# A ring of raw weights with five places in place of six, and a ring of high parts with five in place of four

## The reference

```python
for l in range(2):                                   # first block
    h = rmsnorm(x, norm_g[l])
    (...) = split_cols(h @ w_in[l])                  # 1024 x 7088: three branches' inputs and their gates
    y_a, y_b, y_c = spatial_gating(...), mla(...), gla(...)
    gates = sigmoid(gate_logits + b_gate[l])
    merged = sum(gates[i] * (y[i] @ w_branch[l, i]) for i in range(3))   # each 512 x 1024
    x = x + merged @ w_out[l]                        # 1024 x 1024
# second block
h = rmsnorm(x); (...) = split(h @ w_in_2)            # 1024 x 3752
y = concat(neighbourhood_attention(...), mlstm(...), gated_deltanet(...))
x = x + y @ w_out_2
x = x + cross_attention(rmsnorm(x), rmsnorm(mem), w_xq, w_xkv, w_xo)
x = x + square(relu(rmsnorm(x) @ w_ff1)) @ w_ff2     # 1024 x 4096, 4096 x 1024
out = rmsnorm(x)
```

## Time and profile before

| | |
|---|---|
| median of 3 runs | 1217.69 us (1217.64 to 1218.66) |
| the profiled execution | 1223.93 us |
| its span, from the first to the last instruction | 1222.2 us |
| busy in the span: TensorE products, VectorE, ScalarE, POOL | 89%, 66%, 47%, 5% |
| read from HBM | 158.11 MB, 130 GB/s over the span |
| granted TensorE clock, mean | 0.93 of full speed |

### The profile page before, as it was taken

How to read it: one execution, slowest core, us unless ns; L and a number is a source line. 1 busy time by engine, 2 the same in 40 slices (tenths; PEclk the granted TensorE clock), 3 DMA queues, 4 the chain that set the end, 5 groups by cost and what they waited for, 6 DMA issues and landing times.

```text
span 1222.2 us, 21915 instructions
## 1 busy us (share of the span) xinstructions
PE 1088.8 (89%) x9048; PEld 991.4 (81%) x9048; DVE 805.3 (66%) x1231; ACT 576.5 (47%) x764; POOL 65.8 (5%) x177
## 2 busy tenths in 40 slices
PE   5999999899999999989858967769977979999996
PEld 5868998899868998989846757769957959999885
DVE  5879666776879667767775565863555665664544
ACT  4665664436575674425242443323312625667332
POOL 3000000100000000501800000000000000000000
PEclk9999999999999999989867975879988989999998
DMA  7644444645644444566342420222023505565552
GB/s 264 180 139 139 127 122 132 213 142 177 179 134 138 136 121 138 173 166 194 92 117 69 138 69 2 70 69 73 4 71 104 184 6 173 173 183 184 189 194 77
DMA packets 71924, 160.58 MB, mean 131 GB/s; under 512 B 5798, under 2 KB 11105, under 8 KB 71825
## 3 DMA queue, kind: packets, MB, share of 16 engines
q1 hardware_dynamic: 68736, 151.05, 40.4%
q0 software_dynamic: 2832, 8.06, 2.2%
q10 hardware_dynamic: 256, 0.08, 0.0%
HBM read 158.11 MB, written 1.05 MB: 130 GB/s over the span
## 4 chain that ended last, share of the span: by engine, by line
PE 72%; DVE 18%; ACT 3%; issue 3%; DMA 3%; ACTq 0%; DVEq 0%
PE psum L434 19%; PE psum L436 18%; PE psum L435 18%; PE psum L786 4%; DVE ring_lo L1116 4%; DMA ring<-in_w_branch 2%; DVE arena L1507 1%; DVE arena L1466 1%; ACT ring_hi L1893 1%; PE psum L672 1%; DVE arena L1468 1%; PE psum L640 1%; PE psum L908 1%; PE psum L618 1%; PE psum L775 1%
## 5 line engine op out<-in xcount | busy, mean ns | idle before, releaser
L1116 DVE TENSOR_TENSOR ring_lo<-ring,ring_hi 128x1024 fp32r<-128x1024 f32 (+5 forms) x292 | 342.6, 1195 | 224.6 <-ACT ring_hi L1893 221.1
L1893 ACT ACTIVATE ring_hi<-ring 128x1024 fp32r<-128x1024 f32 (+5 forms) x292 | 296.6, 1033 | 324.2 <-PE psum L436 298.6
L434 PE MATMUL psum<-hT,ring_hi 128*128 128x256 f32 x1032 | 296.0, 287 | 2.2 <-DVE ring_lo L1116 1.2
L436 PE MATMUL psum<-hT,ring_lo 128*128 128x256 f32 x1032 | 293.8, 285 | 0.0
L435 PE MATMUL psum<-hT,ring_hi 128*128 128x256 f32 x1032 | 293.4, 284 | 0.0
L434 PEld LDWEIGHTS psum<-hT,ring_hi 128*128 128x128 f32 x1032 | 198.9, 193 | 4.3 <-issue 3.8
L436 PEld LDWEIGHTS psum<-hT,ring_lo 128*128 128x128 f32 x1032 | 198.9, 193 | 0.0
L435 PEld LDWEIGHTS psum<-hT,ring_hi 128*128 128x128 f32 x1032 | 198.7, 193 | 0.0
L434 PE MATMUL psum<-ring_hi,hT 128*128 128x512 f32 (+4 forms) x416 | 162.3, 390 | 22.3 <-DVE ring_lo L1116 21.9
L436 PE MATMUL psum<-ring_hi,hT 128*128 128x512 f32 (+4 forms) x416 | 157.7, 379 | 0.0
L435 PE MATMUL psum<-ring_lo,hT 128*128 128x512 f32 (+4 forms) x416 | 157.7, 379 | 0.0
(11 more groups left out here) (423 smaller groups left out, 1427.9 us busy)
## 6 DMA issues: line engine op xcount, KB each, us to landing
ring<-in_w_in SPq DMA_DIRECT2D x120, 512.0 KB, 3.6
ring<-in_w_ff SPq DMA_DIRECT2D x64, 512.0 KB, 3.6
ring<-in_w_branch SPq DMA_DIRECT2D x24, 512.0 KB, 3.4
ring<-in_w_out SPq DMA_DIRECT2D x24, 512.0 KB, 3.5
ring<-in_w_xkv SPq DMA_DIRECT2D x16, 512.0 KB, 3.6
ring<-in_w_in SPq DMA_DIRECT2D x8, 528.0 KB, 3.5
ring<-in_w_xq SPq DMA_DIRECT2D x8, 512.0 KB, 3.5
ring<-in_w_xo SPq DMA_DIRECT2D x8, 512.0 KB, 3.5
```

The source lines that it names most:

```text
L434: mm(b, lhs[0], rhs[0], start=start, stop=False, **how)
L436: return mm(b, lhs[1], rhs[0], start=False, stop=stop, **how)
L1116: V.tensor_tensor(chunk_view(ring_lo, RAW, c), chunk_view(ring, RAW, c), plain(chunk_view(ring_hi, RING_HI, c)), ALU.subtract).then_inc(ev ...
L1893: AC(chunk_view(ring_hi, RING_HI, c), chunk_view(ring, RAW, c), ACT.Copy).then_inc(ev("whi_ready"), 1)
```

## The change

One place of 4224 bytes in each partition moves from the ring of raw weights to the ring of high parts. The sum of both stays ten places, and every buffer behind them keeps its address. No instruction is added or removed. What changes are the places that the chunks go to and two waits: chunk c's load waits for the release of chunk c - 5 and no longer of c - 6, and its high part for the release of c - 5 and no longer of c - 4. At the start of the kernel five loads and no longer six are issued without a wait.

```diff
 FF = 4096
 CHUNKS = 4
 CHUNK_W = KD // CHUNKS * 528
-RAW, RING_HI = 6, 4
+RAW, RING_HI = 5, 5
```

## The result

The changed kernel is slower. Its runs have a median of 1223.64 us (1222.73 to 1226.1, 5 runs) against 1217.64 us (1214.52 to 1218.66, 5 runs) of the kernel before; the ratio is 1.0077, 95% interval 1.0050 to 1.0105. A second comparison gave 1.0057 (1.0036 to 1.0079). The profiled execution took 1223.82 us for a span of 1222.1, which is where that of before was (1223.93 and 1222.2). So the two traces, laid side by side as wholes, show no difference at all, while the runs show 5 to 9 us. The reason lies in the trace of before, and is told with the first experiment.

The account below looks back on a forecast made before the run. TensorE (72% of the chain) bounds; weight-pipeline steps matter only where it or VectorE's chain waits. Losses 10.5 us less gains 7.3 make 3.2 us slower: 1227.1 us profiled, 1220.9 us in the runs, range 1215.6 to 1225.6.

Parts of the forecast that it names:

- Which wait decides: All chunks: splits wait for the load issued at the release of c-5, about 0.7 us later; free from 1007 us.
- the split behind the second layer's branch loads: Sign in the changed profile: this split waits longest of all, with a transfer over 9 us on the chain.
- The gains: Splits between q and k squares lose waits at 74.2 and 350.81 us, together 6.2 us; with 596.78 us, 7.3 us.
- the small chunk at 597 us: A 128x256 chunk's split at 596.78 us starts at 595.65 instead: gain 1.1 us.
- The first layer's burst: POOL's ten loads, 229 to 235 us: the chain's chunk lands at 242.5 instead of 239.8, 2.7 us lost.
- the split at 255 us: Split at 255.08 us waits for a load landing at 256.1: 0.3 to 1.0 us lost, 0.7 taken.
- rival (c): Second layer's burst costs the full 6.3 us, clock falls in first layer too: 7.8 us, 1225.5 us; chance 0.13.
- The second layer's burst: Landing at 520.5 instead of 514.2 us, 6.3 us; partly recovered at the next load: 3.8 us lost, bounds 1.9 to 6.3.
- The two splits at 297 us: At 297.04 us the second split waits for a load until 298.4 instead of 297.8: 0.6 us lost.
- Then four of one kind: Last splits of four ahead of ScalarE's copies at 681.07, 716.86, 832.77 and 975.56 us: together 2.7 us lost.
- The base: Whole kernel: 3.2 us added to the profiled 1223.93 us gives 1227.1; the same ratio on the runs' 1217.69 gives 1220.9.
- The clock at the restarts: TensorE restarts at granted 0.51, 539.5 to 546.4 us; less idle time ahead takes 0.4 us off the second layer's loss.

Follow-up runs that it names:

- the first experiment: The kernels before and after run once more without edit: medians 1218.5 and 1224.6 us, profiled executions 1221.36 and 1226.03 us.
- raw5_hi4: Against the kernel after, the fifth high place taken away (five raw, four high places): 1236.0 us, ratio to before 1.0150.
- late_split64: Against the kernel before, ScalarE's single split moved behind the second half's squares, its low part behind the second sum: 1210.4 us, ratio 0.9935.
- again64: The kernel before once more, no edit: 1218.5 us, ratio 1.0008.
- firsts5: Against the kernel before, the first three loads of each group of four in chunks 168 to 227 wait one release more: 1216.0 us, ratio 1.0009.
- second5: Against the kernel before, all loads of chunks 168 to 227 (second block) wait one release more: 1223.7 us, ratio 1.0040.
- lasts5: Against the kernel before, only the last load of each group of four in chunks 168 to 227 waits one release more: 1223.0 us, ratio 1.0063.
- burst5: Against the kernel before, loads of chunks 56 to 67 and 132 to 143, near POOL's bursts, wait one release more: 1226.7 us, ratio 1.0069.
- quiet55: Against the kernel after, POOL's two bursts start later, at the releases of chunks 68 and 144: 1221.6 us, ratio to before 1.0024.
- again55: The kernel after once more, no edit: 1224.6 us, ratio to before 1.0057.

## Why the prediction was off in size

It said slower, by 3.2 us of the profiled time, a ratio of 1.0026, 1220.9 us (1215.6 to 1225.6). The runs' 1223.64 us lie within the range; the ratio is two to three times as far from 1. By its steps:

- **Which wait decides.** Right. With five and five a split starts when a load lands that was issued at the release of c - 5, and the stretches of TensorE from 1007 us on are unchanged. One sign came out otherwise: the split behind the second layer's branch loads does not wait longest. It waits 5.2 us (513.48), the longest wait for a load is 12.7 us (811 us), off the bursts.
- **The gains, 7.3 us.** Right. The q and k stretches went from 30.9 to 27.9 us in both layers (6.0 us for 6.2), and the small chunk at 597 us gave 1.2 for 1.1 (chunks 160 to 164 in 6.1 us in place of 7.3). raw5_hi4 and late_split64 show that it is this wait. TensorE's stream took none of it back.
- **The first layer's burst, 2.7 us, and the split at 255 us, 0.7.** The stretch that holds both takes 4.2 us more (five traces with five raw places have a mean of 70.65 us, six with six 66.42). Measured from TensorE's first product with chunk 52, the load on the chain lands 2.8 us later, as forecast. The split at 255 us comes 0.3 us later, not 0.7, and chunk 65 ahead of it takes 0.4 us more. What the sum lacked is the clock: chunk 60, the first after TensorE's restart, takes 5.2 us in place of 4.3 on average (granted 0.50 in after, 0.63 in again64, 1.00 in firsts5). The prediction had named that this loss may come in the first layer, but priced it in its rival (c) alone.
- **The second layer's burst, 3.8 us.** 2.6 us were measured (70.11 and 67.51), from parts that the sum had sized otherwise. Measured from the first product with chunk 128, the load on the chain lands 5.1 us later, where 6.3 was read; in the six traces with six raw places the two old landings lie 5.5 to 6.7 us apart, so that reading was no chance, but a load issued one chunk later takes 9.4 us and not the 10.5 of its neighbour. 1.9 us come back at the next load, for the 2.1 of the sum. The rest is clock, 0.7 us lost at the first restart and 1.4 gained at the second, told below. The Trainium skill, "DMA: Bandwidth & Descriptors", section "Queues, rings and completion order", has the engines take the queues that have work in turns; the prediction read one chunk, 2.9 us, out of it for this landing. The 5.1 us lie between that and 6.3, and no run here shows the order of single packets.
- **The two splits at 297 us, 0.6 us.** A little too high: chunks 76 to 96 take 0.4 us more in the two traces of after.
- **"Then four of one kind", 2.7 us.** This is the step that failed. The mechanism and the size of one were right (0.7 us each; measured 0.5 to 1.4). The four that it names are chunks 183, 191, 203 and 223: 2.5 us late in after by the table, as forecast, though the last of them costs nothing. But there are nine such groups between 664 and 976 us. I had counted the splits that stand on the chain of the one trace, and a chain shows only the latest of several paths. Together they cost 4.6 us in the traces and 4.9 in the runs of second5. lasts5 and firsts5 show that it is the last split of a group that counts.
- **Left out:** chunks 152 to 160 and 220 to 236, where TensorE starts on products of a new residual, take 0.4 and 0.6 us more. Against it, three long stretches (chunks 28 to 52, 104 to 128 and from 236 on) are shorter by 0.1 each.

The sum with measured terms is 4.2 + 2.6 + 0.4 + 4.6 + 1.0 less 0.3 and 7.2, or 5.3 us slower, a ratio of 1.0044. The prediction's 3.2 us lacks mainly the 1.9 us of the uncounted groups. The comparisons of the runs, 1.0077 and 1.0057, have lower ends of 1.0050 and 1.0036. With the sizes that the runs give for the two places, 8.4 us in burst5 (5.4 to 11.4) and 4.9 in second5 (2.8 to 6.9), the sum is 7.2 us, a ratio of 1.0059, which lies within both intervals; but no stretch of the traces shows the 1.9 us between the two sums, and where they go stays open.

- **The base.** The sum was made against the profiled 1223.93 us, which gave 1227.1 for the profile of after; it took 1223.82. The base was 5 to 6 us too long by chance, as the stretches show. Carrying over only the ratio protected the forecast of the runs from that.
- **The clock at the restarts.** I counted 0.4 us for it in the second layer. The low stretch at 540 us is gone in after: the pair of chunks 142 and 143 takes 5.9 us, not 8.2. The five traces with five raw places there all have 5.9; of the six with six, before has 8.2, four have 7.3 and firsts5 has 5.9. That is 1.3 us on average. Against it chunk 136, the first after the restart at 517 us, takes 0.7 us more (4.3 and 3.6). Further on, chunks 180 and 204 take 4.5 and 4.0 us in after, not 3.0 and 3.1. The same window of before and of after:

```profile
538.00:548.00 10.00, 7.12 (x39) 7.15 (x40) 7.74 (x11) 0.77 (x3) 0.00 (x0) 0.66 0.16 51
```

```profile
538.00:548.00 10.00, 10.00 (x85) 9.85 (x84) 9.56 (x14) 3.08 (x5) 0.00 (x0) 1.00 0.40 143
```

## What to carry to other kernels

A ring's depth decides which event starts each step. Where a step then waits for a transfer instead of a release, count every place where it stands ahead of work that is only nearly on the chain, and not those of one chain alone. Before trading places between rings, look at what a single long wait costs and move the instruction behind it: one moved split gave 7.9 us and took no place from the other ring. And loads that are issued in one burst by another queue are worth spreading out over the releases of the ring that they disturb. A profile is one execution. Repeated profiles of the unchanged kernel would have shown that 5 to 6 us of it were chance; one repeat alone would not, since it was only 2.6 us shorter.

## What was not expected of the hardware

- **Executions of one kernel differ by up to 12 us within one comparison.** 21 runs of before lie between 1214.3 and 1223.9 us, 29 in another comparison between 1212.2 and 1223.8, 18 in a third between 1211.0 and 1219.6. The 11 runs of after lie between 1222.7 and 1226.1, but the 12 of quiet55, also with five and five places, between 1216.4 and 1228.2. The traces show part of where this comes from: the two burst stretches span 3.2 and 5.7 us with six raw places, and 0.9 and 0.4 us with five.
- **The granted clock falls at other chunks in each execution.** The chunk at 143 us took 4.6 us in one trace of before and 3.1 in the other; in again55, burst5 and raw5_hi4 it is the chunk at 190 us that takes 4.6. One such fall costs 1.0 to 1.5 us.
- **Moved to 550 us, the second burst held weight loads up as long as at its old place.** In quiet55 a load on the chain took 12.4 us, with TensorE in a steady stream until then. At the old place the longest load took 12.6 us, but those on the chain 7.7 to 9.4 us.
